# Up-projections with stationary weights: eight 512-column matmuls of a piece first, then its eight 256-column ones

## The chip, the cores and the metric

The program runs on one NeuronCore of a Trainium2 chip, in one launch. The metric is the device time of the launch in microseconds. It holds two transformer blocks at sequence length 256 and model width 2048, all of them in 32-bit floats, so its weights (563 MB read from HBM) pass through the core once.

## What is computed

Both blocks end in a feed-forward part, and the change touches the first matrix product of these parts alone. Cut to that:

```python
D_MODEL, SEQ, D_FF = 2048, 256, 8192

def first_block(...):      # x: (1, 256, 2048)
    ...                    # adaptive norm, two attentions, gates, output projection
    h = _rmsnorm(x, g_pre_ffn[l]) * (1.0 + sc2) + sh2
    f = jnp.square(jax.nn.relu(h @ w_ff1[l])) @ w_ff2[l]
    x = x + gt2 * _rmsnorm(f, g_post_ffn[l])

def second_block(...):
    ...                    # norm, two other attentions, output projection
    h = _rmsnorm_2(x, norm_mlp_pre[layer])
    u = jnp.square(jax.nn.relu(h @ w_up[layer]))
    x = x + _rmsnorm_2(u @ w_down[layer], norm_mlp_post[layer])
```

`w_ff1` and `w_up` are 2048 x 8192, `w_ff2` and `w_down` 8192 x 2048.

## The kernel before

**Arithmetic.** Every float matrix is split in two parts of the type fp32r, a high part and a low one, and a product is made of three matmuls: high by high, low by high, high by low. The split of a weight is made on the core as it streams in: SyncE brings 1 MB chunks into `raw`, ScalarE copies 1024 columns of it to a high buffer `wh` (line 1419, signal `hi`), and VectorE subtracts to a low buffer `wl` (line 1803, signal `lo`). There are four `wh` and four `wl`, used in turn. A filled pair is a **piece**; ScalarE may refill a pair when TensorE has signalled the end of the piece that lay there before.

**Two ways of multiplying.** In most projections, and in all the down-projections, the activations are stationary and the weights stream past: `bank_mm` (lines 1074, 1075 and 1077) issues three matmuls of 512 columns for each 128 x 512 block of the weights. In the up-projections, all but the first slab of each block ("tall" slabs: 14 of 1024 output columns each), the weights are stationary and the activations stream. The function is `tile`. One tile is 128 output columns by all 256 rows of the sequence and all 2048 input columns, so 16 steps `k` of 128, in two pieces of eight. For each k the first matmul (line 1118) holds a 128 x 128 block of `wh` and streams 512 columns, the high and the low part of the activations `HT[:, k]` side by side: two of the three products at once, laid down in the two halves of one PSUM bank. The second (line 1120) holds the block of `wl` and streams 256 columns, the high part alone, added to the first half of the same bank. There are 14 x 8 = 112 tiles, 224 pieces, 1792 matmuls of either kind.

**Weight loads.** Each matmul has a LDWEIGHTS of its own, which brings the stationary operand into the array. The profile shows these under PEld with the line of their matmul.

**Order around the tiles.** `work_order` writes out one order of work for all engines. A tall slab is eight tiles in a row; between tiles may stand a few matmuls of another task (four transposes of line 1194, which turn rows of modulation factors). After a tile, ScalarE and VectorE take the bank out (lines 1740, 2181, 2187, 1742, 2192), while TensorE goes on with the next of four banks. Tall slabs come in eight stretches of the program: one slab, then three times two slabs in the first block, the same in the second; down-projections lie between them. Before a matmul, TensorE waits for `hi` of its piece, for `lo` of its piece, for the activations, and at the start of a tile for the bank to be empty. Waits that are met already are not repeated.

**A thin case.** `thin` (lines 1097, 1098, 1100) also keeps weights stationary, for two narrow slabs of 80 and 64 columns. It streams only 256 columns in each of its matmuls, 48 in a row for each slab.

Of the kernel before, what the change touches and what calls it, by code (L numbers as in the profile page):

```python
# [718 lines left out]
def build(nc, stream, vecs, rows, consts, masks, x_in, pos_in, out):  # L719
# [8 lines left out]
    def signal(name):  # L728
        made.append(Signal(sem(name)))
        return made[-1]  # L730
# [44 lines left out]
    hi, evac_a, high, scaled = signal("hi"), signal("evac_a"), signal("high"), signal("scaled")  # L775
# [3 lines left out]
    lo, acc, summed, mods = signal("lo"), signal("acc"), signal("summed"), signal("mods")  # L779
# [7 lines left out]
    events, items, pieces = work_order()  # L787
# [19 lines left out]
    def piece_memory(p):  # L807
        slot, w = pieces[p]["slot"], pieces[p]["w"]
        if isinstance(slot, int):
            return wh[slot][:, 0:w], wl[slot][:, 0:w]  # L810
        if slot[0] == "M":
            v = MR[:, 2048 * slot[1]:2048 * slot[1] + 2048]
            return v[:, 0:w], v[:, 1024:1024 + w]
        buf, k = {"HT": HT, "U": U}[slot[0]], 8 * slot[1] + 4 * slot[2]
        v = buf[:, k:k + 4, :, :].rearrange("p k h n -> p (k h n)")
        return v[:, 0:w], v[:, 1024:1024 + w]
# [40 lines left out]
    def lhs(name, k, t):  # L857

        p = name[:2]
        if p in ("ya", "yb"):  # L860
            return (U[:, k], ("o", "A", k)) if p == "ya" else (U[:, 8 + k], ("o", "B", k))
        if p == "wo":
            return (U[:, 8 + k] if k < 8 else HT[:, k - 8]), ("mix", k)
        if p in ("uq", "uk"):
            k0 = 0 if p == "uq" else 4
            return U[:, 8 + k0 + k], ("lat", k0 + k)
        if p in ("oa", "ob"):
            return U[:, k], ("o", "D", k) if k < 8 else ("o", "M", k - 8)
        if p in ("fd", "gd"):
            g = int(name[2])  # L870
            return U[:, k - 16 * g], ("u", p[0], g, k - 16 * g)
        c = 1 if p == "fu" else 3 if p == "gu" else 2 if name in ("c2", "kr2", "q2", "k2", "v2") else 0
        return HT[:, k], ("h", c, k, t)
# [179 lines left out]
    def tensor(e):  # L1053
# [50 lines left out]
        def tile(name, ps, i):  # L1104


            o = bank[i % 4]
            for s, k in free[i % 4]:
                e.wait_ge(*s(k))
            for p in ps:  # L1110
                H, L = piece_memory(p)
                for j, k in enumerate(pieces[p]["ks"]):
                    for t in range(2):
                        a, ready = lhs(name, k, t)
                        e.wait_ge(*halves(ready))
                    c = slice(128 * j, 128 * j + 128)
                    e.wait_ge(*hi(p))
                    e.matmul(o[:, :], H[:, c], a.rearrange("p h n -> p (h n)"), start=k == 0, stop=False)  # L1118
                    e.wait_ge(*lo(p))
                    ins = e.matmul(o[:, 0:256], L[:, c], a[:, 0, :], start=False, stop=k == 15)  # L1120
                ins.then_inc(*gemm.tick(("piece", p), *([(name, i)] if p == ps[-1] else [])))
            free[i % 4] = [(evac_v, (name, i))]
# [265 lines left out]
        for kind, *what in work_of(items, "PE"):  # L1388
            if kind == "bank":
                bank_mm(*what)  # L1390
            elif kind == "thin":
                thin(*what)
            elif kind == "tile":
                tile(*what)
            elif kind == "colsum":
                column_sums(*what)
            elif kind == "presum":
                first_column_sums(*what)
            elif kind == "rowvec":
                row_vec(*what)  # L1400
            elif kind == "xturn":
                x_turn(*what)
            elif kind == "turn":
                turn(*what)
            elif kind == "seg" and what[0][0] in tasks:
                tasks[what[0][0]](*what)
# [957 lines left out]
```

## Time and profile before

| | |
|---|---|
| median of 3 runs | 2588.19 us (2587.95 to 2591.11) |
| profiled execution, span from first to last instruction | 2589.9 us |
| instructions in it | 30579 |
| TensorE matmul (PE) busy | 2553.1 us, 99% |
| TensorE weight loads (PEld) busy | 2111.5 us, 82% |
| VectorE (DVE) busy | 1732.6 us, 67% |
| ScalarE (ACT) busy | 1209.1 us, 47% |
| GpSimd (POOL) busy | 6.4 us |
| DMA | 567.11 MB, mean 219 GB/s |
| mean granted TensorE clock | 0.998 of full |

For the profiled execution the page has no other time than its span, 2589.9 us; that is 1.7 us over the median of the runs. Its busy time for PE counts a matmul from its start to a modelled end, and consecutive matmuls overlap in it: a matmul of 512 columns is shown as about 0.39 us long while the next one starts 0.23 us after it. What a matmul costs in a stream is therefore read from the distance between starts, either from a timeline or by counting the instructions in a long window.

### The profile page before, as it was taken

Reading aid. Unit: us, or ns where it says so; the run is one execution under the profiler, and the core shown is the slowest. Engines: PE = TensorE matmul, PEld = TensorE weight load, DVE = VectorE, ACT = ScalarE, POOL = GpSimd, SP = SyncE. Lnnn points to the kernel's source line nnn. Section 1 sums busy time; section 2 is a strip of 40 time slices with the busy share of each in tenths; the row PEclk is TensorE's granted clock in tenths of the full one; section 3 lists DMA queues with packets and bytes.
Section 4 is the critical chain, followed back from the end, with each engine's and each line's share of the span. In section 5 each row is a group of like instructions: output and inputs, shape, how many; then the busy total and the mean of one; then the engine's idle time right before and its main releaser. Section 6 shows DMA issues by size and latency. Waiting matters only on the chain.

```text
span 2589.9 us, 30579 instructions
## 1 busy us (share of the span) xinstructions
PE 2553.1 (99%) x12374; PEld 2111.5 (82%) x12374; DVE 1732.6 (67%) x2308; ACT 1209.1 (47%) x1743; POOL 6.4 (0%) x16
## 2 busy tenths in 40 slices
PE   7999999999999999999999999999999999999998
PEld 4887788887777888888888888878788888888887
DVE  5887988788886866556556565546665565564665
ACT  4534445443346444435434465445564343443443
POOL 0000000000000000000000000000000000000000
PEclk9999999999999999999999999999999999999999
DMA  9994367498885785555555545533555555555453
GB/s 361 381 354 167 122 245 276 180 343 314 332 330 215 263 304 188 197 190 186 205 181 184 206 171 180 194 116 145 195 179 195 180 193 197 180 195 194 179 197 145
DMA packets 80764, 567.11 MB, mean 219 GB/s; under 512 B 9024, under 2 KB 9152, under 8 KB 16112
## 3 DMA queue, kind: packets, MB, share of 16 engines
q1 hardware_dynamic: 79488, 558.09, 58.9%
q0 software_dynamic: 1136, 7.07, 0.7%
q8 instruction: 98, 1.61, 0.2%
q14 instruction: 42, 0.34, 0.0%
HBM read 563.02 MB, written 2.10 MB: 218 GB/s over the span
## 4 chain that ended last, share of the span: by engine, by line
PE 87%; DVE 8%; DMA 3%; ACT 2%; issue 1%; SPq 0%; DVEq 0%; ACTq 0%
PE ps L1074 19%; PE ps L1077 19%; PE ps L1075 19%; PE ps L1118 16%; PE ps L1120 8%; DVE wl L1803 3%; DMA raw<-stream_in 2%; DVE ACC L1824 2%; ACT wh L1419 1%; DMA X<-x_in 1%; PE ps L1359 1%; DVE M L2144 1%; PE ps L1335 0%; PE ps L1194 0%; PE ps L1136 0%
## 5 line engine op out<-in xcount | busy, mean ns | idle before, releaser
L1803 DVE TENSOR_TENSOR wl<-raw,wh 128x1024 fp32r<-128x1024 f32 x845 | 996.7, 1220 | 564.8 <-ACT wh L1419 563.8
L1419 ACT ACTIVATE wh<-raw 128x1024 fp32r<-128x1024 f32 x845 | 847.1, 1049 | 715.2 <-PE ps L1077 579.6
L1118 PE MATMUL ps<-HT,wh 128*128 128x512 f32 x1792 | 633.0, 398 | 0.0
L1074 PE MATMUL ps<-wh,U 128*128 128x512 f32 x1376 | 538.2, 391 | 0.0
L1077 PE MATMUL ps<-wl,U 128*128 128x512 f32 x1376 | 536.4, 390 | 0.8 <-DVE wl L1803 0.5
L1075 PE MATMUL ps<-wh,U 128*128 128x512 f32 x1376 | 535.6, 389 | 0.0
L1120 PE MATMUL ps<-HT,wl 128*128 128x256 f32 x1792 | 503.3, 281 | 0.5 <-DVE wl L1803 0.5
L1074 PE MATMUL ps<-wh,HT 128*128 128x512 f32 x1096 | 438.1, 400 | 6.7 <-DVE M L2144 2.5
L1077 PE MATMUL ps<-wl,HT 128*128 128x512 f32 x1096 | 429.6, 392 | 1.9 <-DVE wl L1803 1.9
L1075 PE MATMUL ps<-wh,HT 128*128 128x512 f32 x1096 | 427.6, 390 | 0.0
L1118 PEld LDWEIGHTS ps<-HT,wh 128*128 128x128 f32 x1792 | 336.5, 188 | 81.8 <-DVE M L2181 0.2
L1120 PEld LDWEIGHTS ps<-HT,wl 128*128 128x128 f32 x1792 | 338.6, 189 | 1.8 <-DVE wl L1803 1.1
L1077 PEld LDWEIGHTS ps<-wl,U 128*128 128x128 f32 x1376 | 258.2, 188 | 57.7 <-DVE wl L1803 3.4
L1075 PEld LDWEIGHTS ps<-wh,U 128*128 128x128 f32 x1376 | 258.4, 188 | 53.1 <-issue 0.2
L1074 PEld LDWEIGHTS ps<-wh,U 128*128 128x128 f32 x1376 | 258.3, 188 | 53.0 <-issue 0.2
L1074 PEld LDWEIGHTS ps<-wh,HT 128*128 128x128 f32 x1096 | 206.2, 188 | 55.5 <-DVE M L2144 6.2
L1077 PEld LDWEIGHTS ps<-wl,HT 128*128 128x128 f32 x1096 | 205.9, 188 | 50.9 <-DVE wl L1803 7.1
L1075 PEld LDWEIGHTS ps<-wh,HT 128*128 128x128 f32 x1096 | 206.4, 188 | 40.2 <-issue 0.5
L1824 DVE SCALAR_TENSOR_TENSOR ACC<-raw,VT,ACC 128x1024 f32<-128x1024 f32 (+3 forms) x176 | 220.8, 1255 | 9.1 <-DMA raw<-stream_in 5.0
L1740 ACT ACTIVATE M<-ps 128x256 f32<-128x256 f32 x112 | 43.1, 385 | 206.2 <-PE ps L1120 206.2
L1742 ACT ACTIVATE U<-M 128x256 fp32r<-128x256 f32 x112 | 46.8, 418 | 139.9 <-DVE M L2187 139.9
L2181 DVE TENSOR_TENSOR M<-ps,M 128x256 f32<-128x256 f32 x112 | 47.5, 424 | 56.9 <-ACT M L1740 56.2
(275 smaller groups left out, 1381.0 us busy)
## 6 DMA issues: line engine op xcount, KB each, us to landing
raw<-stream_in SPq DMA_DIRECT2D x497, 1024.0 KB, 4.8
raw<-stream_in SPq DMA_DIRECT2D x16, 896.0 KB, 6.6
raw<-stream_in SPq DMA_DIRECT2D x17, 640.0 KB, 7.2
raw<-stream_in SPq DMA_DIRECT2D x13, 512.0 KB, 4.1
M<-rows_in POOLq DMA_DIRECT2D x6, 1024.0 KB, 7.0
y_out<-X SPq DMA_DIRECT2D x3, 512.0 KB, 2.6
X<-x_in SPq DMA_DIRECT2D x1, 1024.0 KB, 6.0
X<-x_in SPq DMA_DIRECT2D x2, 512.0 KB, 14.3
```

The lines of the kernel that those rows point to most:

```text
L1074: e.matmul(o, ah, H[:, c:c + bw], start=k == k0, stop=False)
L1075: e.matmul(o, al, H[:, c:c + bw], start=False, stop=False)
L1077: ins = e.matmul(o, ah, L[:, c:c + bw], start=False, stop=end)
L1118: e.matmul(o[:, :], H[:, c], a.rearrange("p h n -> p (h n)"), start=k == 0, stop=False)
L1120: ins = e.matmul(o[:, 0:256], L[:, c], a[:, 0, :], start=False, stop=k == 15)
L1359: ins = e.matmul(s1, QKT[:, 128:256], QKT[:, 256:512], start=True, stop=not rope_key)
L1419: e.activation(H, raw[place[n][0]][:, c:c + w], ACT.Copy).then_inc(*hi.tick(p))
L1740: e.activation(z, bank[i % 4][:, 256:512], ACT.Copy).then_inc(*evac_a.tick((name, i)))
L1742: e.activation(d[:, 0, :], z, ACT.Copy).then_inc(*high.tick(key))
L1803: e.tensor_tensor(L, raw[place[n][0]][:, c:c + w], H.bitcast(F32), ALU.subtract).then_inc(*lo.tick(p))
L1824: e.scalar_tensor_tensor(a, r, cs, a, ALU.mult, ALU.add).then_inc(*acc.tick(key))
L2181: e.tensor_tensor(z, p[:, 0:256], z, ALU.add).then_inc(*evac_v.tick((name, i)))
```

## The change

In `tile`, the one loop over the eight steps of a piece becomes two. The first waits for `hi` of the piece and issues the eight 512-column matmuls. The second waits for `lo` and issues the eight 256-column matmuls. The wait for `hi` now stands ahead of those for the activations, and the wait for `lo` comes after eight matmuls instead of one. Nothing else is different: the same instructions, the same operands, the same signals.

```diff
@@ -1109,14 +1109,17 @@
                 e.wait_ge(*s(k))
             for p in ps:
                 H, L = piece_memory(p)
+                e.wait_ge(*hi(p))
                 for j, k in enumerate(pieces[p]["ks"]):
                     for t in range(2):
                         a, ready = lhs(name, k, t)
                         e.wait_ge(*halves(ready))
                     c = slice(128 * j, 128 * j + 128)
-                    e.wait_ge(*hi(p))
                     e.matmul(o[:, :], H[:, c], a.rearrange("p h n -> p (h n)"), start=k == 0, stop=False)
-                    e.wait_ge(*lo(p))
+                e.wait_ge(*lo(p))
+                for j, k in enumerate(pieces[p]["ks"]):
+                    a, _ = lhs(name, k, 0)
+                    c = slice(128 * j, 128 * j + 128)
                     ins = e.matmul(o[:, 0:256], L[:, c], a[:, 0, :], start=False, stop=k == 15)
                 ins.then_inc(*gemm.tick(("piece", p), *([(name, i)] if p == ps[-1] else [])))
             free[i % 4] = [(evac_v, (name, i))]
```

Two places in TensorE's order show it. The first is the start of the first tall slab (834 us in the profile). `ps0` is the bank, `wh0` and `wl0` are the buffers of the piece; `s_hi`, `s_lo` and `s_evac_a` are the signals of ScalarE's split, VectorE's split and the emptied bank. Before:

```order
L1077 MATMUL ps3<-wl3,HT 128x512
L1118 MATMUL ps0<-HT,wh0 128x512 [waits s_hi,s_evac_a]
L1120 MATMUL ps0<-HT,wl0 128x256 [waits s_lo]
L1118 MATMUL ps0<-HT,wh0 128x512
L1120 MATMUL ps0<-HT,wl0 128x256
```

And after, where line 1120 has become line 1123:

```order
L1077 MATMUL ps3<-wl3,HT 128x512
L1118 MATMUL ps0<-HT,wh0 128x512 [waits s_hi,s_evac_a]
L1118 MATMUL ps0<-HT,wh0 128x512 x7
L1123 MATMUL ps0<-HT,wl0 128x256 [waits s_lo]
L1123 MATMUL ps0<-HT,wl0 128x256 x7
L1118 MATMUL ps0<-HT,wh1 128x512 [waits s_hi]
```

The wait for `s_lo` has moved behind seven more matmuls, and kinds of matmul no longer alternate within a piece. The second place is between the fourth and the fifth tile of that slab (858 us), where four transposes (line 1194, then 1197) stand between two tiles. Before:

```order
L1120 MATMUL ps3<-HT,wl3 128x256
L1194 MATMUL ps7<-CT,M 128x128 x4
L1118 MATMUL ps0<-HT,wh0 128x512 [waits s_hi,s_evac_v]
L1120 MATMUL ps0<-HT,wl0 128x256 [waits s_lo]
L1118 MATMUL ps0<-HT,wh0 128x512
```

After:

```order
L1123 MATMUL ps3<-HT,wl3 128x256 x7
L1197 MATMUL ps7<-CT,M 128x128 x4
L1118 MATMUL ps0<-HT,wh0 128x512 [waits s_hi,s_evac_v]
L1118 MATMUL ps0<-HT,wh0 128x512 x7
L1123 MATMUL ps0<-HT,wl0 128x256 [waits s_lo]
```

The transposes have kept their place between the tiles, and here too the wait for `s_lo` comes seven matmuls later. The orders of the other four engines' instructions are the same as before.

## Rows read from the trace of the kernel before

**Rows 1.** The page: span, busy times, and the chain that ended last
```profile
span 2589.9 us, 30579 instructions
...
PE 2553.1 (99%) x12374; PEld 2111.5 (82%) x12374; DVE 1732.6 (67%) x2308; ACT 1209.1 (47%) x1743; POOL 6.4 (0%) x16
...
PE 87%; DVE 8%; DMA 3%; ACT 2%; issue 1%; SPq 0%; DVEq 0%; ACTq 0%
PE ps L1074 19%; PE ps L1077 19%; PE ps L1075 19%; PE ps L1118 16%; PE ps L1120 8%; DVE wl L1803 3%; DMA raw<-stream_in 2%; DVE ACC L1824 2%; ACT wh L1419 1%; DMA X<-x_in 1%; PE ps L1359 1%; DVE M L2144 1%; PE ps L1335 0%; PE ps L1194 0%; PE ps L1136 0%
```

**Rows 2.** Windows, stretches of tall slabs: start:end length, PE busy, clock, DMA, GB/s
```profile
834.16:881.95 47.79, 47.25 (x273) 1.00 0.74 275
...
2225.36:2315.80 90.44, 90.44 (x514) 1.00 0.52 183
...
sum 637.37, PE 636.83; mean PE 79.60
```

**Rows 3.** Windows of line 1118 alone: length, PE busy (count), PEld busy (count)
```profile
1176.00:1238.00 62.00, 62.00 (x180) 33.47 (x179) 1.00 0.57 200
2226.00:2314.00 88.00, 88.00 (x250) 46.81 (x250) 1.00 0.52 183
```

**Rows 4.** Timeline, matmuls of a steady tile: start us, length us, engine, line
```profile
1000.06 0.40 PE L1118 MATMUL ps<-HT,wh 128*128 128x512 f32 x1
1000.29 0.28 PE L1120 MATMUL ps<-HT,wl 128*128 128x256 f32 x1
1000.41 0.40 PE L1118 MATMUL ps<-HT,wh 128*128 128x512 f32 x1
```

**Rows 5.** Timeline, weight loads of the same matmuls
```profile
1000.06 0.19 PEld L1120 LDWEIGHTS ps<-HT,wl 128*128 128x128 f32 x1
1000.30 0.19 PEld L1118 LDWEIGHTS ps<-HT,wh 128*128 128x128 f32 x1
1000.41 0.19 PEld L1120 LDWEIGHTS ps<-HT,wl 128*128 128x128 f32 x1
```

**Rows 6.** Window of a down-projection, line 1074 of its three (512 columns each)
```profile
1080.00:1140.00 60.00, 34.39 (x89) 16.51 (x88) 1.00 0.55 195
```

**Rows 7.** Timeline, plain fp32 operands in the attention, 512 and 256 passes
```profile
378.72 0.59 PE L1335 MATMUL ps<-ACC,M 128*128 128x256 f32 x2
379.15 0.38 PE L1336 MATMUL ps<-ACC,M 128*128 128x128 f32 x2
```

**Rows 8.** Windows of PE in the thin slabs (64 columns loaded, then 80)
```profile
1551.70:1556.70 5.00, 5.00 (x46) 1.00 0.24 72
218.30:223.30 5.00, 5.00 (x45) 1.00 0.52 186
```

**Rows 9.** Timeline, weight loads of the thin slab and of four transposes
```profile
1552.22 0.13 PEld L1097 LDWEIGHTS ps<-HT,wh 128*64 128x64 f32 x1
1552.34 0.13 PEld L1098 LDWEIGHTS ps<-HT,wh 128*64 128x64 f32 x1
...
858.18 0.47 PEld L1194 LDWEIGHTS ps<-CT,M 128*128 128x128 f32 x4
```

**Rows 10.** Timeline, from the last tile of a stretch into a down-projection
```profile
1062.83 0.28 PE L1120 MATMUL ps<-HT,wl 128*128 128x256 f32 x1
1062.95 0.40 PE L1074 MATMUL ps<-wh,U 128*128 128x512 f32 x1
...
1064.11 0.39 PE L1077 MATMUL ps<-wl,U 128*128 128x512 f32 x1
```

**Rows 11.** Timeline, PE at the start of the fifth tile of the first slab
```profile
858.65 0.47 PE L1118 MATMUL ps<-HT,wh 128*128 128x512 f32 x1
859.66 0.39 PE L1120 MATMUL ps<-HT,wl 128*128 128x256 f32 x1 [0.54 <-DVE wl L1803]
859.88 0.39 PE L1118 MATMUL ps<-HT,wh 128*128 128x512 f32 x1
860.12 0.28 PE L1120 MATMUL ps<-HT,wl 128*128 128x256 f32 x1
```

**Rows 12.** What ended the idle time before line 1120, whole kernel: us, times
```profile
  DVE wl L1803: 1.6, 3
```

## The prediction, made before the changed kernel was run

> **What bounds the kernel now.** I read the page first, for who sets the end. TensorE is busy 99% of the span and holds 87% of the chain that ended last; lines 1118 and 1120, the only ones that the change moves, hold 16% and 8% of it [rows 1]. So a nanosecond per matmul there counts nearly in full, and the question is how close together TensorE starts these matmuls. Next I read the windows of the eight stretches of tall slabs: together 637.4 us, with the clock granted in full, the DMA half busy, and PE without a gap except 0.5 us in the first stretch [rows 2]. ScalarE, VectorE and the queues keep up there. The stretches are bound by TensorE's own pace.
>
> Then I read the pace. In one long window 250 matmuls of line 1118 touch 88 us; one of them had begun before it, so 249 starts give 353.4 ns for a pair of 512 and 256 columns. In another window 179 starts in 62 us give 346.4 ns [rows 3]. The same instructions with the same clock thus run at two paces. I followed the distances through all eight stretches: of 224 pieces some 34 run at about 346.7 ns a pair (2773 ns a piece), in three blocks, each until the stretch ends, and about 190 at about 353.3 ns (2827 ns). The timeline of the slower pace shows 230 to 240 ns from a 512 to the following 256, and about 120 ns from a 256 to the next 512 [rows 4]. Each weight load begins with the matmul before the one it serves, and its neighbour begins 0.11 us later, before its own 0.19 us are over [rows 5]. So loads run hidden under matmuls, at most about one matmul ahead.
>
> **What one matmul should cost.** 512 and 256 columns at the full 2.4 GHz are 213.3 and 106.7 ns, 320 ns a pair; 26 to 33 ns of each pair is something else. Four places bear on it.
>
> First, down-projections are matmuls of 512 columns alone, each with its load of 128 columns of fp32r. Line 1074 is one of three in turn and 88 of its starts fill 60 us: 60,000 / (3 x 88) = 227 ns [rows 6]. That is 13.5 ns over the columns.
>
> Second, plain fp32 operands, two passes for each column, take 0.43 us for two matmuls of 512 passes, 215 ns each, and 0.11 us for 256 passes [rows 7]: nearly nothing over the columns, although they load 128 columns each.
>
> Third, the thin slabs stream 256 columns of fp32r again and again, with loads of only 64 or 80 columns. Two of the matmuls counted in each window had begun before it: 5000/44 = 113.6 ns and 5000/43 = 116.3 ns [rows 8], so 7 and 10 ns over the columns.
>
> Fourth, the faster pace of the tall slabs, 346.4 ns, is the 320 ns of the columns and twice 13.2 ns.
>
> These agree with one account: with fp32r the load of the next matmul costs the running one about 13.3 ns when it brings 128 columns and about half of that when it brings 64, whatever the length of the matmul. By this account the faster pace is the least that a pair can take, in either order, and the slower pace has 6.7 ns a pair on top. I take that excess for the loads and the two lengths of matmul falling out of step, because it comes and goes in blocks while the work is the same.
>
> The Trainium skill speaks against the account: "TensorE: Matmul & The Clock Gate", section "Step-by-step: what each phase is for", says that loading the next weights does not take read bandwidth from the running matmul, since the two have ports of their own. By it, I estimate, nothing would keep a pair from about 325 ns, from its back-to-back gap of 2.5 ns over the columns. The fp32 rows agree with it and the fp32r rows do not [rows 6, 7].
>
> **The change part by part.** *Matmuls of 512 columns in a row.* They become what the down-projections are, one after another with loads of 128 columns: 227 ns, taken as 226.7 [rows 6]. Eight are 1813 ns.
>
> *Matmuls of 256 columns in a row with loads of 128 columns.* The trace of before has no such run. The lower bound is the thin slab of 64 columns, 113.3 ns; the account gives 106.7 + 13.3 = 120 ns; adding the slower pace's whole excess to it gives 126.7 ns, which I take as the upper bound of the ordinary case. A matmul can't begin before its load has done its part. A load of 64 columns is shown 0.13 us long and one of 128 columns 0.19 us, so 64 more columns cost about 0.055 us and a load streams for some 0.11 us; four loads of transposes lie 0.11 us apart, (0.47 - 0.14) / 3 [rows 5, 9]. That is 10 ns inside the 120, so I take 120 as the nearest value; eight are 960 ns.
>
> *The turns between the kinds.* Where a stretch ends and 512s follow a 256, the first five 512s take 1.16 us, where 5 x 0.2267 would be 1.133 [rows 10]: 27 ns before the stream settles. At the start of a stretch I see no such cost. The change has one turn of each sort in every piece. Bounds 0 and 27 ns; I take 12, below the middle because eight matmuls may be cut off before the five slow ones would follow.
>
> Sum for a piece: 1813 + 960 + 12 = 2785 ns. Before: (190 x 2827 + 34 x 2773)/224 = 2819 ns without the stalls. Gain 34 ns x 224 = 7.6 us.
>
> *The wait for `lo`, moved behind the eighth 512.* Line 1120 waited for VectorE's low part three times, 1.6 us in all [rows 12]. In the largest case the 256 begins 1.01 us after its 512 where 0.24 is normal, 0.78 us late, and the following 256 waits for nothing [rows 11]. After the change the low part is needed 7 x 0.227 = 1.6 us later in its piece, which covers each of these. What is late next would be `hi`, which ScalarE gives over a microsecond before `lo`. Nothing else is queued behind this wait but TensorE's own matmuls. The small losses around the stalls included, I take 1.6 us, between 0 (VectorE is late again as TensorE runs ahead) and 2.1.
>
> *Signals, evacuation and refills.* The piece ends with the same signal, after the same work; ScalarE's refill waits for that as before. The high buffer of a piece could be released earlier but is not. The bank's last matmul is a 256 before and after. I cost these at nothing; the cover is the 2.8 us of a piece against VectorE's 1.2 and ScalarE's 1.0 for a split. All other work is unchanged.
>
> Total: -7.6 - 1.6 = -9.2 us on the span of 2589.9, so 2580.7; on the median, 1.7 us lower, **2579.0 us**.
>
> **The rivals.** *Same (chance 0.27).* What puts the slower pace out of step isn't the alternation but matmuls of 256 with full loads. Then the run of 256s shows about 126.7 ns each, a piece is 1813 + 1013 = 2827 ns or with turns up to 2854, and the gain is the stalls less some 0 to 6 us: 2584 to 2592, likeliest 2587. For it: the slower pace is met in 85% of the pieces, and loads of 80 columns already show 116.3 where 80/128 of 13.3 ns would give 115.0. Against it: blocks at the faster pace have the same 256s.
>
> *Slower (0.13).* In a run of 256s the loads become the bound. Today a load has 120 ns and 235 ns in turn, 353 for two; then it has 120 each time, and what isn't finished can't be caught up. If a load had to be over, 0.19 us, before the next begins, a 256 would take 188 ns, a piece 1813 + 1504 = 3317 ns, and 224 pieces 111.6 us more than 2819: some 2698 us. It decides from where a 256 takes over 129.6 ns, since 1.79 us are added per nanosecond. Against it: loads of 128 columns do start 0.11 us after the one before, and runs of thin loads hold 113 ns [rows 5, 8, 9]; but no run of full fp32r loads does.
>
> *Faster still (0.07).* The 256s run at the thin slab's 113.3 ns: 2720 + 12 ns a piece, 87 less than 2819, so 2588.2 - 19.5 - 1.6 = 2567.
>
> *The whole excess goes (0.03).* If alternation alone causes all of it, a pair takes 215 + 108 = 323 ns as with plain fp32 [rows 7], a piece 2584 ns: 2588.2 - 52.6 - 1.6 = 2534. This is where the Trainium skill's rule above would lead; the down-projections don't alternate and have the excess all the same [rows 6].
>
> **How the numbers follow.** The forecast, 256s at 116 to 123 ns, has 0.50: with turns between 0 and 27 ns it runs from 2570 to 2588, and it lies within 0.2% of before at its upper end. A gain or loss under 0.2%, 5.2 us, is about what a measurement of this kernel can't tell from no change. Of the forecast 0.46 is faster than that and 0.04 isn't. Faster: 0.46 + 0.07 + 0.03 = 0.56, and 0.02 of the rival "same"; same: 0.25 + 0.04 = 0.29; slower 0.13. The range takes in the forecast, the "same" rival and the thin pace: 2565 to 2593. It leaves out the loads as the bound (0.13) and the case in which the whole excess goes (0.03).
>
> **What would show it.** Right: windows of line 1118's runs with 227 ns between starts, of line 1123's with about 120; stretches of tall slabs 628 us together instead of 637.4; no idle time before line 1123 that VectorE ended; the down-projections unchanged at 227 ns. Wrong: 256s at 127 and more, or loads on PEld that begin later than the matmul ahead of theirs; 512s after a turn at over 230 for the whole run; or a wait for `hi` at the start of pieces.

## The result and the profile after

| | before | changed |
|---|---|---|
| median | 2588.36 us (12 runs, 2586.31 to 2591.63) | 2583.14 us (12 runs, 2582.15 to 2584.95) |
| ratio | | 0.9976, 95% interval 0.9968 to 0.9983 |
| span of the profiled execution | 2589.9 us | 2581.7 us |
| eight stretches of tall slabs together | 637.37 us | 630.76 us |

The changed kernel is faster by 5.2 us, 0.24%. Forecast were 9.2 us. The first reading is the page of the changed kernel (span, the busy times, the chain that ended last):

```profile
span 2581.7 us, 30579 instructions
...
PE 2545.9 (99%) x12374; PEld 2113.2 (82%) x12374; DVE 1732.7 (67%) x2308; ACT 1208.7 (47%) x1743; POOL 6.4 (0%) x16
...
PE 84%; DVE 9%; DMA 3%; ACT 2%; issue 1%; SPq 0%; DVEq 0%; ACTq 0%
```

Beside [rows 1] nothing has changed its kind: the same instructions, TensorE at 99%. The 8.2 us between the two spans are more than the medians show, so the difference has to be placed. The windows of the eight stretches of the changed kernel, PE alone (length, busy, count, clock, DMA share, GB/s), answer to [rows 2]:

```profile
831.26:877.73 46.47, 46.47 (x274) 1.00 0.73 279
967.76:1058.83 91.07, 91.07 (x518) 1.00 0.53 193
1145.90:1235.26 89.36, 89.36 (x514) 1.00 0.52 185
...
sum 630.76, PE 630.76; mean PE 78.84
```

The first stretch begins at 831.26 us, 2.90 us earlier than in before's profile [rows 2], and no changed instruction stands ahead of it. In the twelve profiles taken of ten kernels with the same work up to there, this point lies between 828.8 and 841.9 us. So these 2.9 us are chance, and what is left, 5.3 us, is what the medians show. Of it, 6.6 us come from the stretches. Of the time between them, the gap behind the first stretch has grown from 88.84 to 90.03 us, by 1.19, and the other gaps and the tail by 0.1 together. The ordinary gap between two stretches is 87.07 us in both.

The timeline of the changed kernel shows the runs (start, length from the first start to the last modelled end, matmuls of one kind merged). The first answer is the start of the first stretch, the second a piece within a stretch:

```profile
831.26 1.98 PE L1118 MATMUL ps<-HT,wh 128*128 128x512 f32 x8
833.07 0.64 PE L1123 MATMUL ps<-HT,wl 128*128 128x256 f32 x4
```

```profile
1014.14 2.00 PE L1118 MATMUL ps<-HT,wh 128*128 128x512 f32 x8
1015.98 1.11 PE L1123 MATMUL ps<-HT,wl 128*128 128x256 f32 x8
1016.93 0.40 PE L1118 MATMUL ps<-HT,wh 128*128 128x512 f32 x1
```

Here and below, a 512 and a 256 are matmuls of 512 and of 256 columns, and a turn is the change from a run of one kind to a run of the other. Eight 512s take 1.81 us behind another 512 and 1.84 us behind a 256; eight 256s take 0.95 us. The starts in the trace give, in ns, 233, 236, 228, 232, 231, 227, 227, 227 for the 512s after a turn, and 113, 119, then 120 six times for the 256s: 2793 ns a piece. Nearly all pieces of the changed kernel take this, except the first of a stretch (2766) and those behind matmuls of another task, where before had 2827 on average in most and 2773 in some. The second stretch is 1.71 us longer than the third in the changed kernel because four matmuls of another task (line 1185) stand in it: they take 1.31 us, and the 512 behind them 0.40 us more than usual.

### The profile page after: what moved, and what is told of

It is laid out like the page before. It is cut to its first block, busy times and chain, and to the rows that moved or that the text cites. A ratio compares the mean times of both kernels' runs of the same rounds, so it can differ in the third digit from the quotient of the medians.

```text
span 2581.7 us, 30579 instructions
## 1 busy us (share of the span) xinstructions
PE 2545.9 (99%) x12374; PEld 2113.2 (82%) x12374; DVE 1732.7 (67%) x2308; ACT 1208.7 (47%) x1743; POOL 6.4 (0%) x16
## 4 chain that ended last, share of the span: by engine, by line
PE 84%; DVE 9%; DMA 3%; ACT 2%; issue 1%; SPq 0%; DVEq 0%; ACTq 0%
PE ps L1074 19%; PE ps L1077 19%; PE ps L1075 19%; PE ps L1118 15%; PE ps L1123 8%; DVE wl L1806 3%; DVE ACC L1827 3%; DMA raw<-stream_in 2%; ACT wh L1422 1%; DVE M L2147 1%; DMA X<-x_in 1%; PE ps L1362 1%; PE ps L1338 0%; PE ps L1197 0%; PE ps L1139 0%
## 5 line engine op out<-in xcount | busy, mean ns | idle before, releaser
L1118 PE MATMUL ps<-HT,wh 128*128 128x512 f32 x1792 | 449.6, 393 | 0.0
L1118 PEld LDWEIGHTS ps<-HT,wh 128*128 128x128 f32 x1792 | 322.8, 189 | 58.6 <-DVE M L2184 0.2
L1123 PEld LDWEIGHTS ps<-HT,wl 128*128 128x128 f32 x1792 | 244.5, 190 | 17.4
L1123 PE MATMUL ps<-HT,wl 128*128 128x256 f32 x1792 | 249.9, 282 | 0.0
```

## The experiments

Ten experiments follow: eight new kernels, one of them measured twice, and the changed kernel again. The unchanged parts of the program served as a control: in each kernel the undisturbed gap between two stretches is 87.0 to 87.1 us, so a difference of 0.3 us in a stretch stands out although the medians can't show it.

**1. One turn for each tile instead of two.** The edit, in short: the second piece of a tile issues its 256s first.

```diff
-                e.wait_ge(*hi(p)); eight 512s of p; e.wait_ge(*lo(p)); eight 256s of p
+                runs = [(hi, highs), (lo, lows)] if p == ps[0] else [(lo, lows), (hi, highs)]
+                for m, (part, run) in enumerate(runs):
+                    e.wait_ge(*part(p))
+                    for j, (d, w, a, first) in enumerate(run):
+                        ins = e.matmul(d, w, a, start=first, stop=p == ps[-1] and m == 1 and j == 7)
```

> The changed kernel, but in the second piece of each tile the eight 256-column matmuls come first and the eight 512-column ones after them. Theory A (turns): what a piece loses is the turn from 256 to 512 columns, 27 ns over five matmuls, less 7 ns gained by the first 256 after a 512; half of the turns are gone, so a stretch of 32 pieces takes 89.36 - 16 x 0.020 = 89.04 us, the 512s after the turn inside the second piece show 233, 236, 228, 232, 231 ns, and those at the start of a tile 227. Theory B (pieces): the first 512s of a piece are slow because the piece is new (its wait, its buffer); then the 512s in the middle of the second piece run at 227 from the first on and those at the start of each tile stay slow. The whole kernel gains 2.2 us on the changed one under A, about the same under B by another path; the distances tell them apart.

Measured: 2582.26 us, ratio to before 0.9968 (0.9959 to 0.9978); before itself had 2590.80 us beside it, over 2 us more than in the other comparisons. A stretch of this kernel and the sum of the eight, then its timeline from the start of one (three answers):

```profile
1146.99:1236.06 89.07, 89.07 (x514) 1.00 0.52 185
...
sum 629.06, PE 629.06; mean PE 78.63
```

```profile
1146.99 1.98 PE L1124 MATMUL ps<-HT,wh 128*128 128x512 f32 x8
1148.81 2.08 PE L1124 MATMUL ps<-HT,wl 128*128 128x256 f32 x16
1150.72 1.32 PE L1124 MATMUL ps<-HT,wh 128*128 128x512 f32 x5
```

```profile
1152.56 1.98 PE L1124 MATMUL ps<-HT,wh 128*128 128x512 f32 x8
```

```profile
1154.37 1.12 PE L1124 MATMUL ps<-HT,wl 128*128 128x256 f32 x8
```

The eight 512s in the middle of the second piece begin at 1150.72 and the next tile's at 1152.56: 1.84 us, with the single distances 234, 235, 229, 232, 231, 227, 226, 227 ns. Those of the next tile, a new piece in a new bank, take 1.81. The slow 512s follow the turn and not the piece. Theory A holds, and its 89.04 us were 89.07.

**2. The wait for the low part ahead of the 512s.**

```diff
+                e.wait_ge(*lo(p))
                 for j, k in enumerate(pieces[p]["ks"]):
...
-                e.wait_ge(*lo(p))
```

> The changed kernel, but the wait for the low part stands ahead of the eight 512-column matmuls, beside the one for the high part. Theory A: the later wait hid VectorE's lateness in the first stretch of tall slabs only to give it back in the down-projection behind it (stretch 1.33 us shorter, gap behind it 1.19 us longer in the changed kernel than before), so here the stretch takes again some 47.6 us, the gap some 88.9 us, and their sum stays within 0.3 us of the changed kernel's 136.5. Theory B: the later wait gained 1.3 us and the longer gap has another cause; then the stretch takes 47.6 us or more, the gap stays 90.0, and the sum is 137.6 or more. All other stretches as in the changed kernel, 89.36 us for 32 pieces.

Measured: one run, 2587.78 us. The first stretch and the start of the second, then the waits of the changed kernel in the gap behind its first stretch (waiting engine and line, what it waited for, us in total, times, longest):

```profile
833.68:881.75 48.07, 47.02 (x273) 1.00 0.74 273
970.59:1061.66 91.07, 91.07 (x518) 1.00 0.53 192
```

```profile
PEld ps L1077 <- DVE wl L1806: 1.5, 2, 0.9
PE ps L1077 <- DVE wl L1806: 0.6, 2, 0.5
```

The stretch takes 48.07 us and the gap 88.84 (881.75 to 970.59). The sum is 136.9, against 136.5 for the changed kernel and 136.6 for before. The two wait rows stand in neither before's gap nor this kernel's. So the later wait did hide VectorE's lateness, and TensorE then reached the down-projection before VectorE had its low parts. In the other kernels the sum hardly moves either, whatever their pace: 46.20 + 90.28 = 136.5 us in experiment 5, which has the shortest pieces of all, 136.5 to 136.7 in the rest. VectorE sets the time over stretch and gap together, and the changed kernel gained 0.1 us there against before. The expectation had the sum within 0.3 us of 136.5 and it was 0.4 off; theory B needed 137.6 or more. The expectation also missed the third stretch, which was to stay at 89.36 us:

```profile
1148.73:1238.48 89.75, 89.58 (x513) 1.00 0.51 184
```

There too TensorE waited for VectorE's low part, 0.2 us by the profile, and the changed order has no such wait. A wait ahead of all 512s asks for the low part one 512 earlier than before's order does, so this kernel bounds what the later wait is worth and does not give it exactly.

**3. and 4. Groups of two and of four.** The loop over eight becomes `for g in range(0, 8, 2)` (or 4), with the 512s of a group and then its 256s.

> The changed kernel with groups of two instead of eight: two 512s, two 256s, four times in a piece. Theory A1 (each turn costs its full 20 ns net): a piece takes 2773 + 4 x 20 = 2853 ns, a stretch of 32 pieces 91.3 us. Theory A2 (a turn's cost is laid on the 512s one after another, 6.3 on the first and 9.3 on the second, and the first 256 gives 7 back): 2773 + 4 x 9 = 2809 ns, 89.9 us. Rival (cost of alternation as such, the more kinds alternate the more it costs): between the changed kernel's 89.36 and before's 90.44.

> The changed kernel with groups of four: four 512s, four 256s, twice in a piece. Groups of two took 2787 ns a piece, groups of eight 2793. From the distances of the run of eight: the first four 512s after a 256 take 930 ns (23 over 4 x 226.7), the four 256s after them 113 + 119 + 120 + 120 = 472; 2 x 1402 = 2804 ns, a stretch of 32 pieces 89.7 us. A rival that only counts turns (20 ns net for each) gives 2773 + 40 = 2813 ns, 90.0 us; one that interpolates between groups of two and eight gives 89.2 to 89.3.

Measured: 2586.18 us and 2585.04 us, one run each. A stretch of 32 pieces and the timeline in it, groups of two first, then groups of four:

```profile
1326.07:1415.23 89.16, 89.16 (x513) 1.00 0.52 186
```

```profile
1354.62 0.63 PE L1121 MATMUL ps<-HT,wh 128*128 128x512 f32 x2
1355.09 0.39 PE L1127 MATMUL ps<-HT,wl 128*128 128x256 f32 x2
1355.32 0.62 PE L1121 MATMUL ps<-HT,wh 128*128 128x512 f32 x2
```

```profile
1322.14:1411.93 89.79, 89.79 (x514) 1.00 0.52 183
```

```profile
1350.18 1.09 PE L1121 MATMUL ps<-HT,wh 128*128 128x512 f32 x4
1351.11 0.64 PE L1127 MATMUL ps<-HT,wl 128*128 128x256 f32 x4
```

Groups of two take 2787 ns a piece: all three readings offered for them were wrong. The two of theory A were too high, and so was the rival, which gave more than 89.36 us a stretch. Two 512s and two 256s take 0.70 us here, the 256s 0.23: the two 256s take 116 and 113 ns or 113 and 119, the two 512s 233 and 236 or 232 and 231, in turn. Groups of four take 2807 ns a piece; adding up the distances seen in the run of eight had given 2804, and counting turns 2813. There the fourth 512 takes 224 ns in every second group, where the run of eight has 232. So the place behind the last turn alone does not give a matmul's time; where the runs are shorter than the five matmuls in which a stream settles, the sum has to be measured. More turns do not mean more time: with four turns to the 512s a piece takes 2787 ns, with two 2807, with one 2793, and with one in two pieces (experiment 1) 2783.

**5. and 6. Fewer stationary columns.** Both are the changed kernel with `c = slice(128 * j, 128 * j + 64)` and `o[0:64, ...]`, or with one column and `o[0:1, ...]`. They leave out half, or all but one, of the output columns of each tile; the streams keep their length.

> The changed kernel with only 64 of the 128 stationary columns in each matmul of the tall slabs: half of each tile's output columns is not computed. Theory L (the load of the next matmul costs the running one 13.3 ns for 128 columns, in proportion to the columns): 512s at 220 ns, 256s at 113.3, a piece 2667 ns without turns and up to 2687 with, a stretch of 32 pieces 85.3 to 86.0 us. Rival R (fp32r streams at 16/17 of the column rate whatever is loaded): 512s at 226.7 and 256s at 113.3 or as before at 120, a stretch of 88 to 89.4 us.

> The changed kernel with one stationary column in each matmul of the tall slabs, so almost no load: 127 of each tile's 128 output columns are not computed. Theory L (what a matmul of fp32r takes over its columns is the price of the load under it): 512s at 213 to 215 ns, 256s at 107 to 109, a piece 2560 to 2590 ns, a stretch of 32 pieces 82 to 83 us. Rival R (fp32r streams slower than its columns by 1/16 whatever is loaded, and only the 256s with full loads wait for a load): 512s at 227, 256s at 113, a piece 2720 ns, a stretch 87.1 us. The run with 64 columns, 88.3 us, speaks for R.

Measured: 2575.33 us and 2576.58 us, one run each. A stretch and a piece of the kernel with 64 columns; a stretch, a piece and a load of the one with a single column:

```profile
1319.03:1407.35 88.32, 88.32 (x514) 1.00 0.53 187
```

```profile
1346.63 2.00 PE L1118 MATMUL ps<-HT,wh 128*64 128x512 f32 x8
1348.47 1.08 PE L1123 MATMUL ps<-HT,wl 128*64 128x256 f32 x8
1349.39 1.08 PE L1118 MATMUL ps<-HT,wh 128*64 128x512 f32 x4
```

```profile
1318.59:1407.32 88.73, 88.73 (x513) 1.00 0.53 186
```

```profile
1346.31 2.01 PE L1118 MATMUL ps<-HT,wh 128*1 128x512 f32 x8
1348.16 1.09 PE L1123 MATMUL ps<-HT,wl 128*1 128x256 f32 x8
1349.08 1.08 PE L1118 MATMUL ps<-HT,wh 128*1 128x512 f32 x4
```

```profile
1346.77 0.08 PEld L1118 LDWEIGHTS ps<-HT,wh 128*1 128x1 f32 x1 [0.15 <-issue]
```

The load of one column is shown 0.08 us long instead of 0.19, and the piece takes 2773 ns: exactly the faster pace of before, with full loads. With 64 columns it takes 2760. The eight 512s take 1.85 us with one column (225 to 235 ns each) and 1.84 with 64: no less than with 128. Theory L, on which the prediction's price of 120 ns rested, has fallen: it gave 213 to 215 ns for a 512 with one column.

The 256s are another matter. Eight of them take 0.92 us in both kernels and 0.95 with full loads. By the starts in the trace the first four take 113 to 120 ns and the last four 113 to 114, with 64 columns as with one, where they settle at 120 with 128. The thin slabs, 48 in a row with 64 columns, held the same 113.6 ns [rows 8]. So a full load does hold a run of 256s back, by some 6.5 ns each, but between 64 columns and one nothing more is gained. Rival R had this part right, 113 for the settled 256s. As a whole it falls too: it gave 87.1 us for the single column and 88.7 came, because the 512s there never settle at 227 but take 231 on average.

What is seen throughout is some 13 ns over the columns for each matmul of fp32r on average, 26.7 for a pair, in the single-column kernel, in before's faster pace and in the down-projections [rows 6], and nearly nothing with plain fp32 [rows 7]. What the engine does in these 13 ns stays open.

**7. Tipping the alternating order into its faster pace.** In before, the pace went over from 353.3 to 346.7 ns a pair in the middle of a stretch, twice right behind a piece whose first load of the low part came late without the matmul being late. The weight loads and matmuls of before at one such place (two answers):

```profile
870.72 0.19 PEld L1118 LDWEIGHTS ps<-HT,wh 128*128 128x128 f32 x1
870.98 0.19 PEld L1120 LDWEIGHTS ps<-HT,wl 128*128 128x128 f32 x1
```

```profile
870.83 0.40 PE L1118 MATMUL ps<-HT,wh 128*128 128x512 f32 x1
871.07 0.29 PE L1120 MATMUL ps<-HT,wl 128*128 128x256 f32 x1
```

The load at 870.98 begins 0.15 us after the matmul it lies under, where 0.003 is usual; the pieces behind take 2773 ns to the end of the stretch. The other places are in the fifth stretch, and no late load stands there: the pace changes behind each of three groups of four transposes, to the faster one at 1926 us, back at 1932 and to the faster one again at 1938. The edit brings such a shift about in before's order: the 256-column matmul of the second step of a slab is issued as two of 128 columns.

```diff
+                    if k == 1 and i == 0:
+                        for q in range(2):
+                            ins = e.matmul(o[:, 128 * q:128 * q + 128], L[:, c], a[:, 0, 128 * q:128 * q + 128], start=False, stop=False)
+                    else:
                         ins = e.matmul(o[:, 0:256], L[:, c], a[:, 0, :], start=False, stop=k == 15)
```

> The alternating order of before, but at the second step of each slab the 256-column matmul is issued as two of 128 columns on the same weights, so that the loads come later against the matmuls by some 0.1 us, as they did in before when VectorE's low part came just late, at 870.8 and 1172.6 us. Theory P (the alternating order has two self-holding paces, 353.3 and 346.7 ns a pair, and which of them it keeps is a matter of the phase of loads and matmuls): if the nudge tips it, pieces take 2773 ns and a stretch of 32 pieces 88.8 to 88.9 us, the kernel some 8 to 9 us under before. If this nudge isn't the right one: 90.5 us a stretch, like before. Rival (the faster pace came from something else in those stretches, a buffer or a lighter load of the DMA): 90.5 us in every stretch but the third and parts of the first and fifth, which stay as in before.

Measured: 2584.04 us, ratio 0.9977 (0.9968 to 0.9987). Stretches that had 90.44 us in before have 88.96. The second stretch fell back to the slower pace behind the four matmuls of another task (line 1186) at 995 us, and was tipped again at the start of its second slab. The fifth, 46.46 us in before, came out slower: its nudged pace ended at the first transposes, and its second half, at the faster pace in before, has the slower one here:

```profile
978.52:1069.74 91.22, 91.22 (x519) 1.00 0.54 193
1333.02:1421.98 88.96, 88.96 (x516) 1.00 0.52 186
1919.73:1966.61 46.88, 46.88 (x274) 1.00 0.48 168
```

Theory P holds in its main part: there are two paces, each keeps itself up, and one split matmul tips the stream from the one into the other, while buffers, DMA and all other instructions are before's. The rival gave 90.5 us there. That the two paces differ in the phase of loads against matmuls is not shown: in both, each load begins 2 to 5 ns after the start of the matmul that it lies under. What differs is the distances, 236, 113, 233, 117, 241, 120 ns over and over in the slower pace and 230 and 117 in the faster. A wait alone does not end the faster pace: at 1179 us TensorE waits 0.2 us for VectorE's low part, that piece takes 2967 ns, and those behind it 2773 again. The kernel gained 4.7 us in the median where 8 to 9 were expected, since the first, the second and the fifth stretch did not keep the faster pace.

**8. to 10. The changed kernel, the order with one turn, and a single nudge for each stretch**, measured side by side on one chip. The last is experiment 7 with the condition `and (name[3] == "0" or name[2] == "0")` added.

> The changed kernel itself once more, as the measure for the two beside it. Stretches of tall slabs as in its first profile (89.36 us for 32 pieces, 89.36 + 1.7 where TensorE waits for the activations), 5.2 us under before in the median. The start of the first tall slab, which no changed instruction precedes, lay between 828.8 and 841.9 us in the profiles so far; if the 2.9 us by which it came earlier in the first profile of the changed kernel are chance, it lies anywhere in that range here.

> The order with one turn for each tile, once more, beside the changed kernel. Its profile had 89.07 us for 32 pieces against 89.36, in all 1.7 us less in the stretches. Theory A: 1.7 us under the changed kernel in the median too, ratio to before 0.9973 or less; the medians can hardly tell 1.7 us apart.

> The alternating order with the nudge only in the first slab of each stretch. Theory P: the faster pace, once tipped, holds over the end of the slab until something disturbs it; 32 pieces take 2773 x 32 + 0.1 = 88.85 us, in a stretch whose pieces wait for nothing, and the sum of the stretches is 0.2 to 1 us under that of the order with one turn for each tile. Rival: without the nudge the second slab of a stretch falls back to 2827 ns a piece, then 32 pieces take 89.7 us.

| | median | ratio to before | stretches together |
|---|---|---|---|
| before | 2587.89 us | | 637.37 us |
| changed | 2582.79 us | 0.9982 (0.9973 to 0.9991) | 630.77 us |
| one turn for each tile | 2580.67 us | 0.9974 (0.9964 to 0.9983) | 629.06 us |
| one nudge for each stretch | 2583.91 us | 0.9979 (0.9970 to 0.9988) | 631.08 us |

The stretches repeat to 0.01 us from one profile of a kernel to the next: 630.76 and 630.77, 629.06 and 629.06. The first began at 830.02 us in the changed kernel here, within the range named. The expectation's "waits for the activations" is wrong: the 1.7 us of the second stretch are the four matmuls of line 1185 and the late start behind them. In the kernel with one nudge (a stretch, then the timeline at its start, with the two halves on line 1122):

```profile
1326.32:1415.17 88.85, 88.85 (x514) 1.00 0.53 186
```

```profile
1326.66 0.40 PE L1118 MATMUL ps<-HT,wh 128*128 128x512 f32 x1
1326.89 0.33 PE L1122 MATMUL ps<-HT,wl 128*128 128x128 f32 x2
1327.07 0.45 PE L1118 MATMUL ps<-HT,wh 128*128 128x512 f32 x1
1327.35 0.28 PE L1124 MATMUL ps<-HT,wl 128*128 128x256 f32 x1
```

The nudge costs 0.1 us at 1327 and the faster pace holds for the other 31 pieces, over the end of the slab: 88.85 us, as expected. It doesn't hold in the second stretch (91.95 us), and the alternating order keeps its stalls in the first (47.80 us). That makes its sum 631.08, more than the 629.06 of the order with one turn, which was expected to be the larger. By the traces the order with one turn is the best of all complete kernels here, 1.7 us under the changed one in the stretches; its two medians lie 8.5 and 7.2 us under before's beside them, the first with before's high median of 2590.80. Against the changed kernel in the same rounds it is 2.1 us, in accord with the trace, but the intervals of the two ratios overlap.

## Why the prediction was right, and where it wasn't

*Direction and range: right.* 2583.1 lies between 2565 and 2593, and the sign is the forecast one, with 5.2 us where 9.2 were forecast. The range says little, since it holds before's own 2588.4 as well; the tests of the prediction are its terms.

*TensorE's pace sets the time: right.* Each nanosecond taken from the tall slabs came through to the end, but for the first stretch. The down-projections and the gaps kept their time, except the gap behind that stretch.

*The pace of the 512s: right.* A run of them takes 227 ns each, once settled, as read from [rows 6].

*The 256s at 120 ns: right in size, wrong in its reason.* They take 120 ns from the third on. The account behind it, 13.3 ns for a load of 128 columns and half of that for 64, "whatever the length of the matmul", fell with the single stationary column (experiments 5 and 6). The step that failed is "with fp32r the load of the next matmul costs the running one about 13.3 ns": the thin slabs of [rows 8] were read as a scale in loaded columns for matmuls of any length, and they are not one. A 512 gets no shorter with 64 columns or one; a settled 256 takes 113 to 114 ns with either and 120 with 128. So of the 13.3 ns over its columns some 6.5 come with a full load and the rest with any load, and that the account's sum met 120 is in part luck. 2773 ns a piece, by the account the least with full loads in either order, was not undercut by any kernel with full loads; 64 columns gave 2760.

The Trainium skill ("TensorE: Matmul & The Clock Gate", "Step-by-step: what each phase is for") says that loading the next weights takes no read bandwidth from the running matmul. For the 512s the trace agrees, 1.84 or 1.85 us for eight with any load; where the 6.5 ns come from that a full load adds to a 256, no run here shows. The 2.5 ns over the columns that the same section gives back-to-back matmuls are not met by any fp32r matmul here: they take 13 ns over them on average, and the settled 256s under small loads 7.

*The turns: mis-sized.* Bounds 0 and 27 ns were right; the 12 ns taken were too few. A turn to the 512s costs the whole 27 ns, since all five slow ones fit in a run of eight, and the prediction's reason for less ("eight matmuls may be cut off before the five slow ones would follow") doesn't bear on a run longer than five. The turn to the 256s gives 7 back. Net 20: 8 ns more than taken, 1.8 us over 224 pieces. The stretches' pace gave (2819 - 2793) x 224 = 5.8 us instead of 7.6.

*The later wait for `lo`: mechanism right, worth wrong.* No idle time before line 1123 is left that VectorE ended, and the stretches gained 0.8 us more than by the pace. The 1.6 us of [rows 12] were read wrongly: they add the idle time of the loads and that of the matmul, which for the largest case are one wait (in before's first stretch, engine and line, what it waited for, us in total, times, longest):

```profile
PEld ps L1120 <- DVE wl L1803: 1.1, 2, 0.9
PE ps L1120 <- DVE wl L1803: 0.5, 1, 0.5
```

By the starts only two 256s were late, by 0.78 and 0.18 us. But 1.2 us came back in the gap behind the first stretch, as a wait of line 1077 for VectorE (experiment 2). The prediction named `hi` as the next to be late; it was VectorE's `lo` again, in the down-projection right behind the stretch. Its sentence on the lower bound, "VectorE is late again as TensorE runs ahead", was the case. The term was -1.6 and came out at +0.5 with the 0.1 of the other gaps.

The sum with these terms: -5.8 - 0.8 + 1.2 + 0.1 = -5.3 us, the difference of the two profiles from the first tall slab to the end.

*The rivals.* "Slower" was excluded by the first 256s: full loads in a run begin 0.12 us apart, and the 256s take 120 ns and no more. "Same", 256s at 127 ns, didn't come, although the gain lies near the 0.2% that the prediction took for the least measurable one. Its own numbers do not follow from its sum: pieces of 2827 to 2854 ns with the stalls gone give 2588 to 2594 us, not 2584 to 2592. "Out of step", the prediction's word for the 6.7 ns, is half shown: the alternating order can be tipped between its paces without touching what it computes (experiment 7), but no row shows that the loads are what falls out of step. Of its three blocks at the faster pace, "each until the stretch ends", the one in the fifth stretch is broken for two pieces by transposes.

## What to carry to other kernels

Read a matmul stream's cost from the distances between starts, over long windows and over each place after a change of shape. The same two instructions took 346.7 or 353.3 ns here by what went before them alone, and an order that removes the slower pace can bring in turns that cost nearly as much: the change took 54 ns a piece away and gave 20 back. Where a wait is moved later on the engine that bounds, ask whether the engine waited for has any slack until the next place that needs it; if not, the gain comes back there, as 1.2 us did here. To cost a hidden operation, change its size alone (here the stationary columns) before believing a scale read from cases that differ in more than one thing.

## What the runs showed of the hardware that wasn't expected

- A matmul stream of fp32r with alternating lengths of 512 and 256 columns has two self-holding paces, 353.3 and 346.7 ns a pair, at a granted clock of 1.00 in both. One matmul split in two tips it into the faster pace; in before the change came twice behind a load that started 0.15 us late. Matmuls of another task in between (four transposes, or four of line 1186) ended the faster pace, and four transposes also began it; a wait of 0.2 us for VectorE left it as it was. A longer wait for VectorE, 0.5 us at the same place of the first stretch, was followed by the slower pace in before (859.66 us) and by the faster one in the kernel with one nudge (859.99 us). Loads begin 2 to 5 ns after their matmul's start in both paces.
- In runs of eight under full loads: after 256s, 512s take 233, 236, 228, 232 and 231 ns before they settle at 227; after 512s, the first 256 takes 113 ns, the second 119, and the rest 120.
- Loads of 1, 64 and 128 stationary columns under the same streams give pieces of 2773, 2760 and 2793 ns (2773 in the alternating order's faster pace). Fewer loaded columns don't buy shorter 512s of fp32r; a settled 256 takes 120 ns under a load of 128 columns and 113 to 114 under 64 or 1.
- Over the same instructions the length of a stretch repeats to 0.01 us between executions, while the point at which the first one begins moved by 13 us, between 828.8 and 841.9.
